# Prologue of a fused two-block transformer kernel: how the residual, the pool bias, the router weights and the small vectors are loaded

## The chip, the cores and the metric

The kernel runs on one core of a Trainium2 chip. A core has TensorE (PE in the views; its weight loads are PEld), VectorE (DVE), ScalarE (ACT), GpSimd (POOL) and SyncE (SP). SP and ACT issue the transfers here, each on a DMA queue of its own (q1 is SP's, q10 is ACT's), and 16 DMA engines serve both queues. The metric is the device time of the core in microseconds (us), the median over several executions.

## What is computed

One sequence of 256 tokens with 1024 channels in float32 goes through two blocks. Only the beginning of the first one is touched by the change:

```python
def pool_mixer(h, w, b, scale):      # trailing-window means minus the token, per group of 256 channels
    ...
    y = jnp.einsum('bsgc,gcd->bsgd', pooled, w) + b
    return y.reshape(B, S, D) * scale

x = x + pool_mixer(rms_norm(x, pool_norm[l]), pool_w[l], pool_b[l], pool_scale[l])   # layer 0
x = x + hier_moe(rms_norm(x, ffn_norm[l]), router_group_w[l], ..., w_gate[l], w_up[l], w_down[l])
```

`hier_moe` picks one of 4 groups and two of its 8 experts for each token. Layer 1 has multi-head latent attention in place of the pool mixer, and the same expert stage again. The second block (an S5 and an mLSTM branch, cross-attention to a memory `mem_2`, a convolutional feed-forward) follows. Each of the 64 experts has three matrices of 2 MB, which makes some 400 MB of the 512 MB that the kernel moves.

## The kernel before

**Slabs and the ring.** Weights come in slabs of up to 2 MB (128 partitions by 4096 floats). The ring `ring` in SBUF has 6 places; a slab `n` may be loaded (`place_free`, `placed`, L597; `rows`, L579) when the slab that held its place has been used up, which TensorE tells with the semaphore `slabs_done`. Three more slabs of each expert stage (`AHEAD`) go to other memory: one into `arena`, two in halves over X, XN and parts of `arena` (`load_ahead`, `load_over_x` L630, `load_over_sorting` L638). SP issues everything in program order, so a slab that must wait for its place holds back all that stands behind it.

**The prologue.** SP issues `x` into `X` (L538), seven small vectors (`vectors`, L545, of which each is some rows of 128 floats), `pool_w` (L548), the other small vectors, the S5 vectors (L551, L552), the memory (L560), the router's weights and biases of layer 0 (`router_loads`, L555 to L558). Then it waits for `vec2_loaded` and `pool_loaded`, and only then issues slab XK0 (L579) and the first five expert slabs (L597). ACT issues the constants (L1507), the band matrix `inverse_counts` (L1508), the pool bias and the pool scale, both broadcast to 128 partitions (L1509, L1510: 512 KB of writes each), and `ffn_gain` (L1512).

TensorE begins with `keep_busy` (L818, products that nothing reads), transposes the first vectors (L823), goes on with `keep_busy`, and multiplies the normed X with the band (L831, L832) and the result with `pool_w` (L841). DVE copies the transposed gains (L1928), forms XN (L1904), multiplies the product with the scale (L1943) and adds it to X (L1944). GpSimd has by then multiplied bias and scale (L2557) and added them to X (L2564, two instructions of 128x1024).

**Router and experts.** `turn(X)` (L751) makes 16 transposes of 128x128 blocks of X; DVE and ACT copy them with the gain into `hT` (L1913, L1532); the memory is turned in layer 0 as well; L868 multiplies `hT` with the router weights `rw`. The block that is transposed is the operand that a weight load brings in (PEld L751). DVE then picks experts, TensorE sorts the tokens with `XN_rows`, a view of XN with a step of 8 floats, as weights (`sort`, L899), and the expert loop starts: `gate_up` (L956), `turn_hid` (L972), `combine` (L985), `down` (L1000). L1029 is a set of products whose weights have one row.

Of the kernel before, what the change touches and what calls it, by code (L numbers as in the profile page):

```python
# [25 lines left out]
P = 128  # L26
T = 256
TT = T // P
D = 1024
# [55 lines left out]
def side_by_side(widths):  # L85
    at, cols = 0, {}
    for name, n in widths:
# [6 lines left out]
                                    ("iota", SLOTS), ("group", EXPERTS), ("causal_mask", P), ("eps", 1),  # L94
# [4 lines left out]
def constants():  # L99
# [22 lines left out]
    put("eps", np.full((P, 1), EPS))  # L122
# [18 lines left out]
VECTORS = (("pool_norm", 8), ("ffn_norm", 16), ("kv_in_norm", 8), ("attn_norm", 8), ("kv_norm", 2),  # L141
# [117 lines left out]
FIRST_VECTORS = 7  # L259
# [12 lines left out]
def key_tiles(batch):  # L272
# [25 lines left out]
    "proj_mm", "pool_biased",  # L298
# [23 lines left out]
def program(nc, a, out):  # L322
    with ExitStack() as ctx:
# [21 lines left out]
        ffn_gain = sbuf("ffn_gain", [P, 2, KD])  # L345
        PS = ctx.enter_context(nc.psum_tensor("PS", [P, 8, 512], F32))
# [23 lines left out]
        ident, ones, eps = cc("ident"), cc("ones"), cc("eps")  # L370
# [31 lines left out]
        pool_b = ar(13056, D)  # L402
# [4 lines left out]
        hTf = hT[:, :, :].rearrange("p k n -> p (k n)")  # L407
        slots = hTf[:, 0:2 * TOP_K * T].rearrange("p (v n) -> p v n", v=2)
# [128 lines left out]
        def _(sp):  # L537
            sp.dma_start(X[:, :, :], a["x"].rearrange("b (t p) d -> p (b t) d", p=P)).then_inc(s["x_loaded"], 16)  # L538
# [9 lines left out]
            sp.dma_start(pool_w, a["pool_w"].rearrange("a g (c p) d -> p (a g c) d", p=P)).then_inc(s["pool_loaded"], 16)  # L548
            vectors(VEC_PARTS[FIRST_VECTORS:], "vec2_loaded")
            for at, name in ((0, "s5_lam_re_2"), (S5J, "s5_lam_im_2")):  # L550
                sp.dma_start(s5_rows[at:at + S5J, :], a[name][0].rearrange("(j g) p -> j (g p)", g=2)).then_inc(s["s5_loaded"], 16)  # L551
            sp.dma_start(ldt2[32:32 + S5J, :], a["s5_log_dt_2"][0].rearrange("(j g) -> j g", g=2)).then_inc(s["s5_loaded"], 16)  # L552

            def router_loads(layer):
                sp.dma_start(rw[:, :, 0:GROUPS], a["router_group_w"][layer].rearrange("(k p) g -> p k g", p=P)).then_inc(s["row_loaded"], 16)  # L555
# [29 lines left out]
            def experts(layer, n0):  # L585
# [30 lines left out]
                def load_over_x():  # L616

                    name = ("ffn0", "ffn1")[layer]
                    sp.wait_ge(s["x_loaded"], 16 * (2 + 2 * layer))
# [116 lines left out]
        def _(pe):  # L736
# [8 lines left out]
            def turn(v, bank=4):  # L745

                for j in range(KD // 2):
                    for c in (2 * j, 2 * j + 1):
                        for t in range(TT):
                            at = (c % 2) * T + t * P  # L750
                            mm = pe.transpose(PS[:, bank + j, at:at + P], v[:, t, c * P:(c + 1) * P], ident)  # L751
# [71 lines left out]
            pe.transpose(PS[:, 0, 0:FIRST_ROWS], vec_rows[0:FIRST_ROWS, 0, :], ident[0:FIRST_ROWS, 0:FIRST_ROWS]).then_inc(s["vec_turned"], 1)  # L823


            keep_busy(7, 7)
# [8 lines left out]
            pe.wait_ge(s["pool_loaded"], 16 * 3)  # L835
            for g in range(N_POOL):
                pe.wait_ge(s["norm_hT_dve"] if g < 2 else s["norm_hT_act"], KD // 2)
                for t in range(TT):
                    o = PS[:, 2 * t + g // 2, (g % 2) * POOL_GD:(g % 2 + 1) * POOL_GD]
                    for c in range(2):  # L840
                        mm = pe.matmul(o, pl[:, 2 * g + c, t * P:(t + 1) * P], pool_w[:, 2 * g + c, :], start=(c == 0), stop=(c == 1))  # L841
# [3 lines left out]
            def moe(layer, name, n0):  # L845
# [9 lines left out]
                turn(X)  # L855
# [642 lines left out]
        def _(act):  # L1498
# [7 lines left out]

            act.dma_start(const[:, :], a["const"]).then_inc(s["const_loaded"], 16)  # L1507
# [1194 lines left out]
```

## Time and profile before

| | us |
|---|---|
| median of 3 runs (lowest, highest) | 1704.22 (1703.78, 1706.92) |
| the profiled execution: device time | 1701.31 |
| the profiled execution: span of its instructions | 1699.1 |
| PE busy | 1607.1 (95%) |
| DVE, ACT, POOL busy | 456.3, 234.3, 96.7 |
| moved by DMA | 512.48 MB, mean 302 GB/s |

The chain that ended last is TensorE for 63% and DMA for 30%; the DMA part is nearly all the wait for `in_w_up` slabs. The views below are read like this: the chain of waits gives start, length and engine with line of what the end of the program hung on; a stretch gives the busy time of each engine, PE's granted clock, the mean busy share of the 16 DMA engines (it can read slightly over 1) and GB/s.

### The profile page before, as it was taken

To read this page: it belongs to the slowest core of one execution; us is meant where nothing else is said; L and a number is where in the kernel's file an instruction comes from. 1 tells how busy PE (TensorE), PEld (TensorE's weight loads), DVE (VectorE), ACT (ScalarE), POOL (GpSimd) and SP (SyncE) were. 2 spreads that over 40 slices of the span, in tenths; PEclk is the share of its full clock that TensorE was granted. 3 is DMA by queue.
4 is the path that set the end of the run, shared out by engine and by line. 5 is a ranking of instruction groups with operands and counts; after the bars stand their busy time and mean duration, and the time that the engine had idled before them with its cause. 6 is when DMAs were issued, how large, how long until landed. Compare 5 with 4: busy or idle time off the path is not lost.

```text
span 1699.1 us, 22104 instructions
## 1 busy us (share of the span) xinstructions
PE 1607.1 (95%) x9079; PEld 1002.9 (59%) x9079; DVE 456.3 (27%) x982; ACT 234.3 (14%) x519; POOL 96.7 (6%) x165
## 2 busy tenths in 40 slices
PE   8999998888999999999998898899999998999998
PEld 7755544444446756745544444448578667688843
DVE  4311111111113323212111111116976202344411
ACT  4110100000002121101000000012122113100000
POOL 2200000000000000029200000000000000000000
PEclk9999999999999999999999999999999999999999
DMA  9999999999998643899999999999233541444400
GB/s 329 414 423 425 426 427 426 426 425 427 426 421 299 194 173 125 366 408 421 426 426 426 426 426 427 426 380 329 89 124 125 186 161 50 161 149 149 149 25 25
DMA packets 107944, 512.48 MB, mean 302 GB/s; under 512 B 17034, under 2 KB 46315, under 8 KB 74091
## 3 DMA queue, kind: packets, MB, share of 16 engines
q1 hardware_dynamic: 105595, 506.24, 74.3%
q10 hardware_dynamic: 2288, 5.40, 0.9%
q8 instruction: 41, 0.67, 0.2%
q14 instruction: 20, 0.16, 0.0%
HBM read 506.38 MB, written 5.24 MB: 301 GB/s over the span
## 4 chain that ended last, share of the span: by engine, by line
PE 63%; DMA 30%; DVE 4%; SPq 1%; ACT 1%; issue 1%; DVEq 0%; ACTq 0%
DMA ring<-in_w_up 29%; PE PS L956 15%; PE PS L1462 9%; PE PS L1000 5%; PE PS L1224 5%; PE PS L1474 4%; PE PS L1235 2%; PE PS L985 2%; PE PS L899 2%; PE PS L1400 2%; PE PS L1412 2%; PE PS L1389 2%; PE PS L1203 2%; PE PS L811 2%; PE PS L796 1%; DMA ring<-in_x_wkv 1%
## 5 line engine op out<-in xcount | busy, mean ns | idle before, releaser
L956 PE MATMUL PS<-ring,arena 128*64 128x256 f32 x3968 | 449.2, 381 | 54.6 <-DMA ring<-in_w_up 42.5
L956 PEld LDWEIGHTS PS<-ring,arena 128*64 128x64 f32 x3968 | 287.7, 137 | 236.4 <-DMA ring<-in_w_up 59.8
L1000 PE MATMUL PS<-ring,arena 128*64 128x512 f32 x992 | 226.6, 598 | 1.2 <-ACT arena L1641 1.2
L2098 DVE TENSOR_TENSOR arena<-PS,arena 128x256 f32<-128x256 f32 x64 | 27.2, 425 | 719.6 <-ACT arena L1633 719.6
L1000 PEld LDWEIGHTS PS<-ring,arena 128*64 128x64 f32 x992 | 66.2, 136 | 152.8 <-issue 151.3
L1462 PE MATMUL PS<-hT,ring 128*128 128x256 f32 x640 | 138.3, 379 | 0.0
L1462 PEld LDWEIGHTS PS<-hT,ring 128*128 128x128 f32 x640 | 121.6, 190 | 16.5
L985 PE MATMUL PS<-arena,hT 64*128 64x512 f32 x512 | 127.2, 615 | 1.2 <-ACT arena L1650 1.2
L1641 ACT ACTIVATE arena<-PS 128x256 f32<-128x256 f32 x64 | 24.6, 384 | 507.4 <-PE PS L972 507.4
L1224 PE MATMUL PS<-hT,ring 128*128 128x256 f32 x384 | 85.9, 385 | 0.0
L1650 ACT ACTIVATE arena<-PS 128x512 f32<-128x512 f32 x64 | 38.2, 597 | 306.2 <-PE PS L1000 306.2
L1224 PEld LDWEIGHTS PS<-hT,ring 128*128 128x128 f32 x384 | 73.7, 193 | 11.2 <-issue 1.1
L1474 PE MATMUL PS<-ring,arena 128*128 128x512 f32 x176 | 75.7, 592 | 0.0
L985 PEld LDWEIGHTS PS<-arena,hT 64*128 64x128 f32 x512 | 44.1, 186 | 39.9 <-issue 30.2
L1474 PEld LDWEIGHTS PS<-ring,arena 128*128 128x128 f32 x176 | 33.4, 190 | 41.7 <-issue 41.4
L2110 DVE SCALAR_TENSOR_TENSOR hT<-hT,arena 128x512 f32<-128x512 f32 x64 | 50.5, 789 | 0.4 <-PE PS L985 0.2
L2289 DVE SCALAR_TENSOR_TENSOR arena<-PS,VT,arena 128x255 f32<-128x255 f32 (+2 forms) x104 | 43.5, 476 | 1.1
L2284 DVE TENSOR_SCALAR arena<-PS,VT 128x256 f32<-128x256 f32 x48 | 23.0, 538 | 77.5 <-PE PS L1462 77.4
L2092 DVE COPY arena<-arena 128x512 f32 (+1 forms) x64 | 28.6, 447 | 29.2 <-issue 22.2
L972 PEld LDWEIGHTS PS<-const,arena 128*128 128x128 f32 x128 | 20.3, 206 | 24.8 <-issue 24.7
L899 PE MATMUL PS<-arena,XN 128*128 128x256 f32 x128 | 32.3, 409 | 0.9 <-DVE arena L2023 0.9
L899 PEld LDWEIGHTS PS<-arena,XN 128*128 128x128 f32 x128 | 31.2, 335 | 3.2 <-issue 2.9
(422 smaller groups left out, 1433.8 us busy)
## 6 DMA issues: line engine op xcount, KB each, us to landing
ring<-in_w_gate SPq DMA_DIRECT2D x62, 2048.0 KB, 25.5
ring<-in_w_up SPq DMA_DIRECT2D x62, 2048.0 KB, 25.6
ring<-in_w_down SPq DMA_DIRECT2D x62, 2048.0 KB, 24.6
ring<-in_f_w_up SPq DMA_DIRECT2D x22, 1024.0 KB, 6.7
ring<-in_w_in SPq DMA_DIRECT2D x9, 2048.0 KB, 19.1
ring<-in_f_w_down SPq DMA_DIRECT2D x5, 2048.0 KB, 7.9
arena<-in_w_gate SPq DMA_DIRECT2D x2, 2048.0 KB, 23.0
ring<-in_x_wkv SPq DMA_DIRECT2D x2, 2048.0 KB, 8.3
```

The source lines that it names most:

```text
L811: mm = pe.matmul(PS[:, 1, :], hT[:, k, t * P:(t + 1) * P], w[:, k, :], start=(k == 0), stop=(k == KD - 1))
L899: mm = pe.matmul(PS[:, 4 * half + c // 2, c % 2 * T:(c % 2 + 1) * T], XN_rows[:, t, c, :], sel[:, t, half * T:(half + 1) * T], start=(t == ...
L956: mm = pe.matmul(PS[half * WINDOW:(half + 1) * WINDOW, bank, m * half_f:(m + 1) * half_f], xw[bank][:, k, :], mat(k, F_EXP)[:, half * half ...
L985: mm = pe.matmul(PS[:, 4 + 2 * t + half, :], buf[rows, t * P:(t + 1) * P], y2[rows, :], start=first, stop=last, skip_group_check=True)
L1000: mm = pe.matmul(PS[half * WINDOW:(half + 1) * WINDOW, 3, :], hidT[:, w, k * WINDOW:(k + 1) * WINDOW], mat(k, D)[:, half * 512:(half + 1) ...
L1203: mm = pe.matmul(PS[:, 2 + 2 * half + t, :], oT[:, h, t * P:(t + 1) * P], w[:, h, :], start=(h == 0), stop=(h == HEADS - 1))
L1224: mm = pe.matmul(PS[:, bank + b, f % 2 * T:(f % 2 + 1) * T], w[:, k, f * P:(f + 1) * P], x[:, k, :], start=(k == 0), stop=(k == kx - 1))
L1462: mm = pe.matmul(PS[:, 2 * (j % 2) + h, f * T:(f + 1) * T], w[:, k, h, f * P:(f + 1) * P], x[:, k, :], start=(k == 0), stop=(k == KD - 1))
L1474: mm = pe.matmul(PS[:, 4 + 2 * t + half, :], gF[:, c, t * P:(t + 1) * P], w[:, c - 4 * j, half * 512:(half + 1) * 512], start=(c == 0), st ...
L1650: act.activation(y2, PS[:, 3, :], ACT.Copy).then_inc(g["y_sbuf"], 1)
L2110: dve.scalar_tensor_tensor(gates2, slots[:, 0, :], slot_of[:, w, bass.ds(linear(e, 1, 0), 1)], slots[:, 1, :], ALU.is_equal, ALU.mult).the ...
L2289: ins = dve.scalar_tensor_tensor(v, ps(f)[:, 0:T - back], taps[f][back], v, ALU.mult, ALU.add)
```

## The change

- `x` is loaded in two halves of one token tile each, the first by SP, the second by ACT, each the first entry of its queue. The constants and the band come after it on ACT's queue.
- Pool bias and pool scale are loaded as one row each. A row of ones (`warm`, a memset in hT) times the scale row gives the broadcast scale in PSUM (two products of 512 columns), which DVE copies to SBUF. A row of ones times the bias row starts the accumulation of the pool product (four products of 512 columns), to which L857 adds. The bias is so inside the product and is scaled with it; GpSimd's three instructions are gone.
- TensorE starts with 8 products of `warm` with itself. After the transposed vectors there are 10 `keep_busy` products (7 before).
- The router weights are loaded with channel `p*8+k` at partition p, part k, which makes each partition's data one run; so `turn(X)` takes its columns with a step of 8 (`X_rows`), in both layers. The gain comes from `ffn_gain` in that order, and `ffn_norm` leaves the list of vectors.
- The second list of vectors and the S5 vectors are issued behind XK0 and the first two expert slabs, and SP's wait before the first slab is gone.
- `eps` is a memset in place of a column of the constants.

```diff
-            sp.dma_start(X[:, :, :], a["x"].rearrange("b (t p) d -> p (b t) d", p=P)).then_inc(s["x_loaded"], 16)
+            sp.dma_start(X[:, 0, :], a["x"].rearrange("b (t p) d -> p (b t) d", p=P)[:, 0, :]).then_inc(s["x_loaded"], 16)
...
-                sp.dma_start(rw[:, :, GROUPS:], a["router_expert_w"][layer].rearrange("(k p) g -> p k g", p=P)).then_inc(s["row_loaded"], 16)
+                sp.dma_start(rw[:, :, GROUPS:], a["router_expert_w"][layer].rearrange("(p k) g -> p k g", p=P)).then_inc(s["row_loaded"], 16)
...
-            sp.wait_ge(s["vec2_loaded"], 16 * (len(VEC_PARTS) - FIRST_VECTORS))
-            sp.wait_ge(s["pool_loaded"], 16 * 3)
...
+                    if layer == 0 and j == SECOND_SLABS:
+                        second_vectors()
                     placed(j)
...
+                            part = v[:, t, c * P:(c + 1) * P] if rows is None else rows[:, t, c, :]
+                            mm = pe.transpose(PS[:, bank + j, at:at + P], part, ident)
...
-            pe.wait_ge(s["const_loaded"], 16)
-            keep_busy(7, 8)
+            pe.wait_ge(s["dve_step"], 2)
+            for _ in range(8):
+                pe.matmul(PS[:, 4, 0:P], warm, warm, start=True, stop=True)
+            pe.wait_ge(s["pool_loaded"], 16 * 2)
+            for half in range(2):
+                mm = pe.matmul(PS[:, 6 + half, :], warm[0:1, :], scale_row[:, half * 512:(half + 1) * 512], start=True, stop=True)
+            mm.then_inc(s["rows_spread"], 1)
+            for half in range(2):
+                for t in range(TT):
+                    pe.matmul(PS[:, 2 * t + half, :], warm[0:1, :], pool_b[:, half * 512:(half + 1) * 512],
+                              start=True, stop=False, skip_group_check=True)
+            pe.wait_ge(s["const_loaded"], 16)
             pe.wait_ge(s["vec_loaded"], 16 * FIRST_VECTORS)
...
-            keep_busy(7, 7)
+            keep_busy(4, 10)
...
-                turn(X)
+                turn(X, rows=X_rows)
...
-            act.dma_start(pool_b, a["pool_b"].rearrange("a g d -> (a g d)").partition_broadcast(P)).then_inc(s["pool_loaded"], 16)
-            act.dma_start(pool_scale, a["pool_scale"][0].partition_broadcast(P)).then_inc(s["pool_loaded"], 16)
+            act.dma_start(X[:, 1, :], a["x"].rearrange("b (t p) d -> p (b t) d", p=P)[:, 1, :]).then_inc(s["x_loaded"], 16)
+            act.dma_start(pool_b, a["pool_b"].rearrange("a g d -> a (g d)")).then_inc(s["pool_loaded"], 16)
+            act.dma_start(scale_row, a["pool_scale"]).then_inc(s["pool_loaded"], 16)
...
-            pool.wait_ge(s["norm_xn"], TT)
-            for t in range(TT):
-                pool.tensor_tensor(X[:, t, :], X[:, t, :], pool_b, ALU.add).then_inc(s["pool_biased"], 1)
```

TensorE's first instructions, before (L818 is `keep_busy`, L823 the transposed vectors, L831 the first band product):

```order
L818 MATMUL PS<-const 128x128 [waits const_loaded]
L818 MATMUL PS<-const 128x128 x7
L823 MATMUL PS<-const,arena 128x53 [waits vec_loaded]
L818 MATMUL PS<-const 128x128 x7
L831 MATMUL PS<-arena,XN 128x256 [waits band_loaded,norm_xn]
```

And after (L828 is the product of `warm`, L831 the scale row, L835 the bias row, L839 the transposed vectors, L847 the first band product):

```order
L828 MATMUL PS<-hT 128x128 [waits dve_step]
L828 MATMUL PS<-hT 128x128 x7
L831 MATMUL PS<-arena,hT 128x512 [waits pool_loaded]
L831 MATMUL PS<-arena,hT 128x512
L835 MATMUL PS<-arena,hT 128x512 x4
L839 MATMUL PS<-const,arena 128x37 [waits vec_loaded,const_loaded]
L824 MATMUL PS<-const 128x128 x10
L847 MATMUL PS<-arena,XN 128x256 [waits band_loaded,norm_xn]
```

Six products of 512 columns now stand ahead of the transposed vectors.

SP's queue from the memory to the third expert slab, before:

```order
L560 DMA arena<-in_mem 128x2x1024
L555 DMA arena<-in_router_group_w 128x8x4
L556 DMA arena<-in_router_expert_w 128x8x32
L557 DMA arena<-in_router_group_b 128x4
L558 DMA arena<-in_router_expert_b 128x32
L579 DMA ring<-in_x_wkv 128x8x384 [waits pool_loaded,vec2_loaded]
L597 DMA ring<-in_w_gate 128x4096
L597 DMA ring<-in_w_up 128x4096
L597 DMA ring<-in_w_gate 128x4096
```

And after, from `pool_w` on:

```order
L551 DMA arena<-in_pool_w 128x8x256
L566 DMA arena<-in_mem 128x2x1024
L561 DMA arena<-in_router_group_w 128x8x4
L562 DMA arena<-in_router_expert_w 128x8x32
L563 DMA arena<-in_router_group_b 128x4
L564 DMA arena<-in_router_expert_b 128x32
L582 DMA ring<-in_x_wkv 128x8x384
L600 DMA ring<-in_w_gate 128x4096
L600 DMA ring<-in_w_up 128x4096
L548 DMA arena<-in_mix_norm_g 8x128
L548 DMA arena<-in_s_d 4x128
```

The slabs follow the router's loads without a wait, and the vectors, which stood ahead of the memory, stand behind two expert slabs.

## Rows read from the trace of the kernel before

**Rows 1.** Chain of waits, first 60 us: start us, length us, what.

```profile
3.64 7.14 DMA arena<-in_mem_norm_g
11.17 3.29 PE PS L818 x14
14.46 0.58 PE PS L831 x2
19.84 6.91 PE PS L841 x32
26.75 2.90 PE PS L818 x26
29.65 3.60 PE PS L751 x32
46.00 8.01 PE PS L899 x32
58.33 7.06 PE PS L956 x64
```

**Rows 2.** Chain of waits, later: both expert stages' bounds, and layer 1's turn.

```profile
235.24 25.78 DMA ring<-in_w_up
507.02 14.01 DMA ring<-in_x_wkv
659.05 1.75 PE PS L751 x16
836.03 22.36 DMA ring<-in_w_up
```

**Rows 3.** Stretches: busy us of the engines, PEclk, DMA share, GB/s.

```profile
20.00:22.00 2.00, 2.00 (x11) 1.77 (x10) 0.00 (x0) 1.74 (x4) 2.00 (x2) 1.00 0.28 33
22.00:24.00 2.00, 2.00 (x11) 1.74 (x11) 0.23 (x2) 1.94 (x7) 2.00 (x1) 1.00 0.69 100
...
232.00:506.00 274.00, 247.46 (x1674) 125.03 (x1672) 37.57 (x77) 23.25 (x56) 0.00 (x0) 1.00 1.01 426
...
668.00:684.00 16.00, 14.40 (x66) 12.74 (x64) 9.09 (x41) 1.73 (x5) 0.00 (x0) 1.00 0.01 4
```

**Rows 4.** Timeline of SP's issues: start us, length, line, transfer.

```profile
87.66 0.43 SPq L638 DMA_DIRECT2D arena<-in_w_down  x1
99.67 0.33 SPq L597 DMA_DIRECT2D ring<-in_w_gate  x1
```

**Rows 5.** SP's own waits between 99 and 100 us.

```profile
SPq L597 <- PE PS L1000: 11.6, 1, 11.6
```

**Rows 6.** Landings, us from issue: issued at 87.66, 99.67, 643.62 and 0.75.

```profile
arena<-in_w_down SPq DMA_DIRECT2D x1, 1024.0 KB, 15.7
ring<-in_w_gate SPq DMA_DIRECT2D x1, 2048.0 KB, 8.6
ring<-in_w_up SPq DMA_DIRECT2D x1, 2048.0 KB, 7.9
const<-in_const ACTq DMA_DIRECT2D x1, 596.5 KB, 5.6
```

**Rows 7.** Timeline of PE and DVE in the prologue; x counts passes, two per product.

```profile
6.39 3.78 PE L818 MATMUL PS<-const 128*128 128x128 f32 x16 [6.39 <-DMA const<-in_const]
12.59 0.75 DVE L1904 TENSOR_SCALAR XN<-X,stat 128x1024 f32<-128x1024 f32 x1
26.58 3.06 PE L818 MATMUL PS<-const 128*128 128x128 f32 x26
```

**Rows 8.** One line's weight loads: ns lowest/median/highest, first and last start.

```profile
L1029 PEld LDWEIGHTS PS<-const,arena x16: 181/187/187, 1140.0 to 1141.7; 1*128 1x128 f32 x16
L899 PEld LDWEIGHTS PS<-arena,XN x128: 312/336/338, 46.0 to 708.4; 128*128 128x128 f32 x128
L751 PEld LDWEIGHTS PS<-const,X x48: 138/140/143, 29.5 to 660.4; 128*128 128x128 f32 x48
```

**Rows 9.** Timeline of DVE and POOL before the pool result is added.

```profile
23.94 0.16 DVE L1937 RECIPROCAL stat<-stat 128x1 f32<-128x1 f32 x1 [1.13 <-ACT stat L1523]
19.37 4.67 POOL L2564 TENSOR_TENSOR X<-X,arena 128x1024 f32<-128x1024 f32 x2
```

More of the change, by code:

```diff
@@ L368, in bc @@
             return v.to_broadcast([P, *shape])
-        ident, ones, eps = cc("ident"), cc("ones"), cc("eps")
+        ident, ones, eps = cc("ident"), cc("ones"), eps_at[:, 0:1]
         ssq, rms, rinv = stat[:, 0:2], stat[:, 2:4], stat[:, 4:6]
@@ L618, in load_over_x @@
                     name = ("ffn0", "ffn1")[layer]
-                    sp.wait_ge(s["x_loaded"], 16 * (2 + 2 * layer))
+                    sp.wait_ge(s["x_loaded"], 16 * (3 + 2 * layer))
                     sp.wait_ge(s["norm_xn"], TT * (SCALED.index(name) + 1))
@@ L743, in slab_wait, with turn @@
                     pe.wait_ge(loaded(n), slab_bytes_due(n))
-            def turn(v, bank=4):
+            def turn(v, bank=4, rows=None):
                 for j in range(KD // 2):
@@ L840, in _ @@
                     for c in range(2):
-                        mm = pe.matmul(o, pl[:, 2 * g + c, t * P:(t + 1) * P], pool_w[:, 2 * g + c, :], start=(c == 0), stop=(c == 1))
+                        mm = pe.matmul(o, pl[:, 2 * g + c, t * P:(t + 1) * P], pool_w[:, 2 * g + c, :], start=False, stop=(c == 1),
+                                       skip_group_check=True)
                     if g % 2:
@@ L1523, in norm, with router_gain @@
                     act.activation(rms[:, t:t + 1], ssq[:, t:t + 1], ACT.Sqrt, bias=eps, scale=1.0 / D).then_inc(s["norm_rms"], 1)
+            def router_gain(layer):
+                return lambda name, c: ffn_gain[:, layer, c:c + 1]
             def hT_upper(name, gains, at=0, dsts=(hT,), bank=4, col=vec):
@@ L1562, in norm_halves @@
                             half(t)
-            act.wait_ge(s["x_loaded"], 16)
+            act.wait_ge(s["dve_step"], 2)
+            act.wait_ge(s["x_loaded"], 32)
+            norm("pool")
             act.wait_ge(s["const_loaded"], 16)
-            norm("pool")
             act.wait_ge(s["vec_ready"], 1)
@@ L1592, in moe @@
                     act.wait_ge(s["hm_moved"], 2)
-                hT_upper(name, ["ffn_norm"], KD * layer)
+                act.wait_ge(s["gain_loaded"], 16)
+                hT_upper(name, ["ffn_norm"], col=router_gain(layer))
                 if layer:
@@ L1904, in norm, with router_gain @@
                         dve.tensor_scalar(XN[:, t, :], src[:, t, :], rinv[:, t:t + 1], None, ALU.mult).then_inc(s["norm_xn"], 1)
+            def router_gain(layer):
+                return lambda name, c: ffn_gain[:, layer, c:c + 1]
             def hT_lower(name, gains, at=0, dsts=(hT,), bank=4, col=vec):
@@ L1924, in scale_turned @@
                        .then_inc(s["h_scaled"], 1)
-            dve.wait_ge(s["x_loaded"], 16)
+            step(dve.memset(eps, EPS))
+            step(dve.memset(warm, 1.0))
+            dve.wait_ge(s["rows_spread"], 1)
+            dve.tensor_copy(pool_scale.rearrange("p (h n) -> p h n", h=2), PS[:, 6:8, :])
+            dve.wait_ge(s["x_loaded"], 32)
             dve.wait_ge(s["vec_turned"], 1)
-            dve.tensor_copy(VT[:, 0:FIRST_ROWS], PS[:, 0, 0:FIRST_ROWS]).then_inc(s["vec_ready"], 1)
+            dve.tensor_copy(VT[:, 0:FIRST_ROWS], PS[:, 5, 0:FIRST_ROWS]).then_inc(s["vec_ready"], 1)
             dve.wait_ge(s["vec_ready"], 1)
@@ L1952, in moe @@
                     dve.wait_ge(s["hm_moved"], 2)
-                hT_lower(name, ["ffn_norm"], KD * layer)
+                dve.wait_ge(s["gain_loaded"], 16)
+                hT_lower(name, ["ffn_norm"], col=router_gain(layer))
                 norm(name)
@@ L2554, in step @@
                 pool.wait_ge(s["pool_step"], steps[0])
-            pool.wait_ge(s["pool_loaded"], 16 * 3)
-            step(pool.tensor_tensor(pool_b, pool_b, pool_scale, ALU.mult))
             pool.wait_ge(s["s5_loaded"], 16 * 3)
```

45 lines of the change are left out of this document (22 added, 23 removed).

## The prediction, written before the changed kernel ran

> **What bounds the kernel now.** I read the chain of waits first, from the start to the second block, then the stretches for the DMA share, then SP's issues with their landings.
>
> Up to 232 us the chain is TensorE and the engines that feed it [rows 1]. From 235 us it is the wait for slabs [rows 2]: in the stretch from 232 to 506 us the 16 DMA engines are busy all the time and move 426 GB/s [rows 3]. Expert stage 0 thus ends when its slab stream ends, and the stage behind it begins with the landing of the slab issued at 507.02, 14.01 us later, at 521.0 [rows 2]. So a prologue counts there only by what it does to that stream. The stream has two possible masters: the moment it starts, and the moments at which TensorE gives back places of the ring. The narrowest such moment is at 99.67: SP had waited 11.6 us for TensorE's L1000 [rows 5], and the transfer issued before that one (87.66) landed 15.7 us later, at 103.4 [rows 4, 6]. The slab issued at 99.67 landed after 8.6 us, at 108.3, 4.9 us behind the one ahead of it, which is what 2 MB take at 426 GB/s [rows 3, 6]. A slab issued into an empty queue, at 643.62, took 7.9 us [rows 6]. So the stream has 8.6 - 7.9 = 0.7 us in hand at 99.67, and no more. A stream that starts earlier has nothing to carry beyond this point unless TensorE comes earlier too; and every us by which TensorE comes later, after the first 0.7, goes into the end of stage 0.
>
> In layer 1 there is nothing in hand: from 668 to 684 us the DMA engines do nothing (share 0.01) [rows 3], since the places wait for TensorE, and the stream bounds the chain again from 836 us [rows 2]. What TensorE loses between 657 and 684 us moves the whole second stage.
>
> **The slab stream's start.** Two broadcasts of 512 KB go: 1.05 MB at 426 GB/s are 2.5 us. The wait of SP goes: shares of 0.28 and 0.69 in two stretches of 2 us are 1.44 + 0.62 = 2.1 us of idle DMA [rows 3]. The router's short runs become long ones; the trace has no row of these alone, I put it between 0 and the 1.5 us that would fill the rest of those stretches. The vectors are only moved. Sum: the stream could start 4.6 to 6.1 us earlier, and no less than TensorE allows. The vectors land behind two slabs, before their first reader (behind L868, at some 37 us), so their move costs nothing; were they late by more than about 5 us, TensorE would stand behind L868.
>
> **TensorE's prologue.** Before, the transposed vectors are done at 11.17, 7 keep-busy products (14 passes) take 3.29 us, and the first band product starts at 14.46 in the chain [rows 1]. XN is ready at 12.59 + 0.75 = 13.34 [rows 7], 2.2 us behind the vectors, because DVE needs these first.
>
> After, TensorE first does 8 products without need of data, from about 1 us to 4.5 us (16 passes took 3.78 us at 6.39 [rows 7]). Then it waits for the two rows. They stand behind half of X on ACT's queue, with the other half of X beside it on SP's: 1 MB ahead of them. The constants, 0.6 MB with as much of X beside them, landed 5.6 us after 0.75 [rows 6], at 6.35. I take 6.2 us.
>
> Price of a product of 512 columns: 16 products of 256 columns take 6.91 us [rows 1], so 0.43 each, 0.86 for 512. That is at the full clock. A keep-busy product takes 3.06/13 = 0.235 us at 26.58, and 3.78/8 = 0.47 us at 6.39 [rows 7]: in the first 14 us TensorE runs at 1.2 GHz, not at 2.4, though the PEclk column reads 1.00. At the low clock 512 columns are 1.72 us. One row of weights is no cheaper than 128: L1029's 16 passes follow each other at (1141.7 - 1140.0)/15 = 0.11 us [rows 8].
>
> When does the clock rise? In the kernel before, near 14.6 us, 8.2 us after the first product and 3.8 us after work resumed from the pause before 10.8 (products behind 14.46 go at full price, those ahead do not [rows 1, 7]). Counted from the first product here this gives 9.3 us, from the resumption at 6.2 it gives 10.0, and if the first 8 products counted for nothing and 8.2 us were needed again, 14.4. I take 11, nearer to the first two.
>
> So: two scale products, 6.2 to 9.6 us. Four bias products: 1.4 us at the low clock do 0.8 of one, the other 3.2 cost 2.75 us, done at 13.75. Transposed vectors, 0.35 us: 14.1. DVE's XN, 2.2 us later: 16.3; 10 keep-busy products at 0.235 end at 16.5. The first band product comes at about 16.5 in place of 14.46: **2.1 us later**. Earlier X and statistics gain nothing, since DVE waits for the vectors, and these for the row products. DVE's own copy of the scale (1024 columns, from 9.6 us) ends before 14.1; it costs nothing unless it took over 4 us.
>
> **GpSimd's bias.** The two additions end at 19.37 + 4.67 = 24.04, and DVE's pool result starts behind them. But DVE also waits for ACT's memory statistics: its reciprocal starts at 23.94 and takes 0.16, so 24.1 [rows 9]. Both waits end together; removing one gains nothing. On TensorE too the 13 keep-busy products run up to the turn at 29.65 [rows 1]. So the 2.1 us pass on unchanged.
>
> **turn(X) with a step of 8.** L751's weight loads take 140 ns, and layer 1's 16 transposes 1.75 us, 0.109 each [rows 2, 8]. The one line that already loads weights with a step of 8, L899, has 336 ns [rows 8], and its 32 passes of 256 columns take 8.01 us, 0.250 each, where L841 with contiguous weights takes 6.91/32 = 0.216 [rows 1]. The first wait aside, L899's loads, not its columns, set 0.24 us. If a transpose of 128 columns is bound by the same load, 16 of them take 3.8 us in place of 1.75: **2.05 us more in each layer**. The lower bound is 0, if the load hides in part behind something that only L899 has. I take 2.05, for L899 is the only such row. In layer 0 the memory's turn and L868 stand behind it, in layer 1 L796 and L868, all in the chain.
>
> The Trainium skill has two sentences that part here. "TensorE: Matmul & The Clock Gate", section "LDWEIGHTS (loading the stationary operand)", lets the load's time hang on the number of columns alone; by that the turn would cost nothing more. "Advanced Engine Details and Errata", section "SBUF Cachelines", says that accesses need two hits on a line of 16 bytes for full speed; a step of 8 floats has one. Rows 8 side with the second.
>
> **The sum.** Stage 0: TensorE is late by 2.1 + 2.05 = 4.15 us at each return of a place; 0.7 is in hand; the stream ends 3.4 us later. The earlier start is all spent by 99.67. Layer 1: 2.05 us. Together 5.45 us. The profiled execution took 1701.31 us (span 1699.1), which becomes 1706.8; the median of 1704.22 lies 2.9 us over it, and becomes **1709.7**.
>
> **Rivals.**
> - *One-row products don't raise the clock.* Then all six cost 1.72: 6.2 + 10.3 = 16.5, vectors at 17.0, ten keep-busy products at 0.47: 21.7. The prologue is 7.2 us late, stage 0 is 8.6 later, sum 10.6: 1714.8. For it: no row has such products at the low clock.
> - *The clock is already up at 6.2 us.* Vectors at 6.2 + 5.2 + 0.35 = 11.75, band product at 14.1, 0.3 early. Stage 0: 2.05 - 0.3 - 0.7 = 1.05, layer 1 2.05, sum 3.1: 1707.3. Against it: 3.8 us of the same products followed by a pause did not do it before.
> - *The step of 8 is free.* Stage 0: 2.1 - 0.7 = 1.4: 1705.6.
> - *The stream's start is the master*, the side opposite to my forecast: if the ring has more in hand than I read at 99.67, the end of stage 0 follows the start. It decides from the point at which the slack there passes 4.15 us. Then -6 to -4.6 us, and +2.05 in layer 1: about 1700.8. For it: the whole of stage 0 past 232 us is DMA, and every byte or gap taken out ahead is real. Against it: SP's wait of 11.6 us for TensorE with only 8.6 us left to the landing.
>
> **Numbers.** Forecast 0.48, low clock 0.17, early clock 0.12, free step 0.10, stream 0.13. A measurement here can tell about 0.2% (3.4 us) from no change. Slower by more: forecast and low clock, 0.65. Within: early clock and free step, 0.22. Faster: 0.13. The range leaves out the stream case and the far end of the low clock: 1703.5 to 1715.
>
> **What would show it.** In the profile of the changed kernel: the first row product near 6.2 us, the band product near 16.5; turn(X) at 0.24 us a transpose in both layers; the first slab landing some 6 us earlier, but an idle DMA before the slab issued near 104 us; 521.0 becoming about 524.4; the second stage another 2 us later. I am wrong if the DMA never idles between 60 and 110 us, if the turn stays at 0.11, or if the band product comes before 14.5.

## The result, and the profile after

The changed kernel takes 1712.65 us (median of 9 runs, 1709.66 to 1715.59), the kernel before 1703.88 us (9 runs, 1702.81 to 1706.92). The ratio is 1.0054, 95% interval 1.0045 to 1.0062: 8.8 us slower, inside the range of the prediction and 3 us above its forecast.

The chain of waits of the changed kernel (start us, length us, what), beside [rows 1]:

```profile
1.76 4.55 DMA arena<-in_pool_scale
...
6.35 1.98 PE PS L831 x4
8.33 6.31 PE PS L835 x8
14.63 0.25 PE PS L839
14.88 4.40 PE PS L824 x20
19.28 0.43 PE PS L847 x2
...
31.43 2.90 PE PS L824 x26
34.33 3.51 PE PS L757 x32
...
50.58 8.04 PE PS L916 x32
58.62 4.32 PE PS L802 x20
62.94 1.87 PE PS L973 x15
64.81 1.15 issue
```

The first band product starts at 19.28 in place of 14.46. The distance from there to the turn (34.33; 29.65 before) and on to the sort (50.58; 46.0 before) is what it was: the 4.8 us of the first 19 pass on as 4.6 to 4.7. The two scale products (L831) cost 0.50 us a pass, the four bias products (L835) 0.79. The stretches of the same kernel (length, then busy us of PE, PEld, DVE, ACT, POOL, then PEclk, DMA share, GB/s) say why:

```profile
6.00:8.00 2.00, 1.65 (x4) 0.85 (x5) 0.00 (x0) 1.99 (x3) 0.00 (x0) 1.00 0.97 346
8.00:10.00 2.00, 2.00 (x4) 0.71 (x3) 1.22 (x1) 1.94 (x6) 0.00 (x0) 0.68 1.00 345
10.00:12.00 2.00, 2.00 (x4) 0.79 (x3) 0.00 (x0) 0.14 (x1) 0.00 (x0) 0.50 1.11 369
...
18.00:20.00 2.00, 2.00 (x13) 1.92 (x13) 0.00 (x0) 0.00 (x0) 0.00 (x0) 0.76 0.79 243
```

The granted clock is at full speed (2.4 GHz) when the row products begin, falls to half (1.2 GHz) in the middle of them, at 8.7 us, and is back only near 19 us. (Ahead of its first rise the PEclk column reads 1.00 as well; that the clock is really up at 6.35 us is seen from the 0.50 us a pass.) From 6.35 us on TensorE is busy all the time; what is unusual is that its products have one row.

At the narrow place, first SP's issue on the timeline, then SP's wait ahead of it, the landing (KB, us from issue), and the stretches around it:

```profile
105.87 0.33 SPq L600 DMA_DIRECT2D ring<-in_w_gate  x1
...
SPq L600 <- PE PS L1017: 11.6, 1, 11.6
...
ring<-in_w_gate SPq DMA_DIRECT2D x1, 2048.0 KB, 7.7
...
104.00:106.00 2.00, 2.00 (x14) 0.79 (x12) 0.00 (x0) 0.12 (x1) 0.00 (x0) 1.00 0.36 147
106.00:108.00 2.00, 2.00 (x22) 1.32 (x20) 0.00 (x0) 0.48 (x1) 0.00 (x0) 1.00 0.73 164
```

The place comes back at 105.87 (99.67 before, [rows 4]) and its slab lands at 113.6 (108.3 before, [rows 6]). The DMA engines run dry here: the stream now waits for TensorE. In the kernel before they were busy in the same stretch:

```profile
104.00:106.00 2.00, 2.00 (x22) 1.35 (x20) 0.00 (x0) 0.00 (x0) 0.00 (x0) 1.00 1.00 426
```

At the end of expert stage 0 the wait that answers to [rows 2] is

```profile
512.08 15.04 DMA ring<-in_x_wkv
```

which lands at 527.1, 6.1 us later than before.

### The profile page after: what moved, and what is told of

Read it like the earlier page. It is cut to its first block, busy times and chain, and to the rows that moved or that the text cites. A ratio compares the mean times of both kernels' runs of the same rounds, so it can differ in the third digit from the quotient of the medians.

```text
span 1710.0 us, 22138 instructions
## 1 busy us (share of the span) xinstructions
PE 1621.5 (95%) x9097; PEld 1010.7 (59%) x9097; DVE 458.2 (27%) x985; ACT 234.2 (14%) x519; POOL 90.0 (5%) x162
## 4 chain that ended last, share of the span: by engine, by line
PE 63%; DMA 30%; DVE 4%; ACT 1%; issue 1%; SPq 1%; ACTq 0%; DVEq 0%
DMA ring<-in_w_up 29%; PE PS L973 15%; PE PS L1479 9%; PE PS L1017 5%; PE PS L1241 4%; PE PS L1491 4%; PE PS L1252 2%; PE PS L1002 2%; PE PS L916 2%; PE PS L1417 2%; PE PS L1429 2%; PE PS L1406 2%; PE PS L817 2%; PE PS L1220 2%; DMA ring<-in_x_wkv 1%; PE PS L802 1%
```

## The experiments

All ratios are to the kernel before, run beside the experiment, with 95% intervals; each trace is one profiled execution. The table puts side by side where the narrowest place comes back (SP's issue that is at 99.67 in [rows 4]), when x_wkv lands, and the time.

| kernel | place back | x_wkv lands | difference | ratio |
|---|---|---|---|---|
| before | 99.7 | 521.0 | 421.3 | |
| router weights and step of 8 alone | 100.3 | 522.2 | 421.9 | 0.9995 |
| broadcasts, vectors first, even rows | 100.5 | 522.7 | 422.2 | 1.0007 |
| the same, bias early | 101.2 | 522.0 | 420.8 | 1.0002 |
| 128 rows, vectors first, even rows | 101.3 | 522.6 | 421.3 | 1.0028 |
| "bias early" with the memory first and the router behind a slab | 101.4 | 522.8 | 421.4 | 1.0016 |
| broadcasts, vectors first | 103.1 | 524.7 | 421.6 | 1.0018 |
| bias behind the vectors | 104.1 | 525.4 | 421.3 | 1.0021 |
| after, even rows | 104.3 | 526.4 | 422.1 | 1.0048 |
| before, 20 more busy products | 104.7 | 526.6 | 421.9 | 1.0030 |
| 128 rows | 104.8 | 526.8 | 422.0 | 1.0041 |
| row products alone | 105.8 | 526.6 | 420.8 | 1.0050 |
| after | 105.9 | 527.1 | 421.2 | 1.0054 |
| broadcasts in after | 106.6 | 527.9 | 421.3 | 1.0036 |

The difference stays between 420.8 and 422.2 while the place moves by 7 us and the first slab's issue ranges from 15.6 to 23.6 us. The ratio follows the place only roughly (101.2 has 1.0002, 101.3 has 1.0028): the medians contain more than stage 0.

### The row products alone, and their opposite

The kernel before with the one-row products and nothing else of the change:

```diff
-            act.dma_start(pool_b, a["pool_b"].rearrange("a g d -> (a g d)").partition_broadcast(P)).then_inc(s["pool_loaded"], 16)
...
+            act.dma_start(pool_b, a["pool_b"].rearrange("a g d -> a (g d)")).then_inc(s["pool_loaded"], 16)
...
+                    pe.matmul(PS[:, 2 * t + half, :], ones[0:1, :], pool_b[:, half * 512:(half + 1) * 512],
+                              start=True, stop=False, skip_group_check=True)
```

> The kernel before with one part alone: the one-row products for pool scale and pool bias ahead of the transposed vectors, GpSimd's additions and the two broadcasts gone; loads of X, router, vectors and SP's wait as before. Theory A: 5.2 us of products at the full clock, 10.3 at the low one, stand ahead of the transposed vectors (11.2 before); the band product comes 3 to 8 us later than 14.5, and the time is 2.5 to 8 us above before. Theory B: the slab stream is untouched, so the time is that of before within 1 us.

Measured: 1713.1 us, ratio 1.0050 (1.0033 to 1.0067). Its chain, and one stretch:

```profile
6.46 3.78 PE PS L818 x16
10.25 1.94 PE PS L824 x4
12.19 5.22 PE PS L828 x8
...
14.00:16.00 2.00, 2.00 (x3) 0.79 (x3) 0.00 (x0) 0.00 (x0) 0.07 (x1) 0.50 1.01 395
```

The clock rose at 10.3 us, about when the row products began, and fell at 13.7 in the midst of them, until 20.5. This part alone loses as much as the whole change (1.0050 and 1.0054, with overlapping intervals).

The changed kernel with the broadcasts and GpSimd's additions put back:

```diff
-                    pe.matmul(PS[:, 2 * t + half, :], warm[0:1, :], pool_b[:, half * 512:(half + 1) * 512],
-                              start=True, stop=False, skip_group_check=True)
...
-            act.dma_start(pool_b, a["pool_b"].rearrange("a g d -> a (g d)")).then_inc(s["pool_loaded"], 16)
...
+            act.dma_start(pool_b, a["pool_b"].rearrange("a g d -> (a g d)").partition_broadcast(P)).then_inc(s["pool_loaded"], 16)
...
+                pool.tensor_tensor(X[:, t, :], X[:, t, :], pool_b, ALU.add).then_inc(s["pool_biased"], 1)
```

> The changed kernel with one part undone: pool bias and pool scale are again broadcast by DMA (behind the band on ACT's queue) and added by GpSimd; no one-row products; all else as changed. Theory A (the six one-row products, priced at the low clock, make TensorE late, and stage 0 follows TensorE): the transposed vectors come near 9 us, the first band product between 11.5 and 13.7 us in place of 19.3, places return 1 to 3 us earlier than in the kernel before, and the time is 0 to 3 us below before (1701 to 1704). Theory B (the slab stream with the vectors behind two slabs is what became slower, since SP stood 11.4 us on one vector transfer): the stream keeps its shape, and the time stays some 6 to 9 us above before.

Measured: 1711.45 us, ratio 1.0036 (1.0024 to 1.0049): little came back. The band product is at 13.1 and the turn at 29.2, but the timeline of PE shows a wait that the changed kernel does not have:

```profile
40.85 0.96 PE L882 MATMUL PS<-const,arena 128*128 128x128 f32 x3 [4.40 <-DMA arena<-in_f_conv_b]
41.91 0.31 PE L886 MATMUL PS<-const,arena 48*128 48x48 f32 x1
42.15 6.08 PE L802 MATMUL PS<-arena,ring 128*128 128x256 f32 x14
```

With TensorE on time, the second vectors behind two slabs are late. SP adds to it: `f_conv_b` is issued only at 36.38 us, behind an issue of `f_conv_w` that holds SP for 11.5 us (more on it below), and no run tells the two shares apart. The wait also lowers the clock (from 37.6 to 47.8 us), so that L802's 14 passes take 6.08 us in place of 3.29, and the sort starts at 52.8, later than in the changed kernel. So the change holds two causes, and one hides the other: TensorE that comes late does not notice vectors that come late.

### The step of 8 alone

```diff
-                sp.dma_start(rw[:, :, 0:GROUPS], a["router_group_w"][layer].rearrange("(k p) g -> p k g", p=P)).then_inc(s["row_loaded"], 16)
+                sp.dma_start(rw[:, :, 0:GROUPS], a["router_group_w"][layer].rearrange("(p k) g -> p k g", p=P)).then_inc(s["row_loaded"], 16)
...
-                turn(X)
+                turn(X, rows=X_rows)
```

> The kernel before with one part alone: router weights in contiguous rows, turn(X) with a step of 8 floats in both layers, gain from ffn_gain. My prediction's step: 2.05 us more in each layer's turn, 3.4 us in all. What the trace of the changed kernel says (1.76 us for 16 passes, as before): nothing, the time is that of before within 1 us, perhaps 1 us less for the shorter router loads.

Measured: 1704.55 us, ratio 0.9995 (0.9985 to 1.0005). The weight loads (ns lowest/median/highest) and layer 1's turn in the chain:

```profile
L754 PEld LDWEIGHTS PS<-const,X x48: 139/192/207, 29.3 to 663.2; 128*128 128x128 f32 x48
...
661.80 1.78 PE PS L754 x16
```

and in the changed kernel

```profile
L757 PEld LDWEIGHTS PS<-const,X x16: 185/188/193, 666.4 to 668.1; 128*128 128x128 f32 x16
...
666.71 1.76 PE PS L757 x16
```

A load is 50 ns longer than in [rows 8], but the 16 transposes take 1.76 to 1.78 us as before ([rows 2]: 1.75). The forecast of 3.8 is refuted.

### A delay of TensorE by itself

```diff
-            keep_busy(7, 7)
+            keep_busy(7, 27)
```

> The kernel before with 20 more keep-busy products behind the transposed vectors, nothing else: TensorE is late by 20 x 0.235 = 4.7 us (up to 9.4 if the clock stays low) in the prologue, the slab stream starts as before. If stage 0's stream has only 0.7 us in hand (my step), the slab whose place returned at 99.67 is issued at 104.4 and lands about 4 us later, and the time is 4 us (up to 8) above before. If the start of the stream is the master, the time is within 1 us of before.

Measured: 1710.61 us, ratio 1.0030 (1.0019 to 1.0042).

```profile
11.31 8.42 PE PS L818 x54
...
51.01 8.01 PE PS L899 x32
```

Sort and place are 5.0 us late, the slab behind the place lands at 112.6, 4.3 late: 0.7 are absorbed there, as read from [rows 6]. At the end of the stage nothing of these 0.7 is left: x_wkv lands at 526.6, 5.6 late.

### 128 rows in place of one

The same number of products of 512 columns in the same places, over 128 rows of constants. This kernel and the next leave out the pool bias and use a scale of one, so they compute something else; only their times and traces are of use.

```diff
-                mm = pe.matmul(PS[:, 6 + half, :], warm[0:1, :], scale_row[:, half * 512:(half + 1) * 512], start=True, stop=True)
+                mm = pe.matmul(PS[:, 6 + half, :], warm, hTf[:, 128:640], start=True, stop=True)
...
-                    pe.matmul(PS[:, 2 * t + half, :], warm[0:1, :], pool_b[:, half * 512:(half + 1) * 512],
+                    pe.matmul(PS[:, 2 * t + half, :], warm, hTf[:, 640:1152],
```

> The changed kernel with its six one-row products replaced by six products over all 128 rows of constants, with as many columns and in the same place (the pool bias is left out and the scale is one; the edit leaves out that part of the computation). TensorE waits for the same two rows of data as before. Theory A (it is the one-row products that let TensorE's granted clock fall at 8.7 us and keep it low until 19 us): the clock stays up from about 5 us on, the six products take 0.86 us each at most, the first band product comes at 14 to 15 us in place of 19.1, the place comes back near 101 us in place of 105.9, and the time is 1704 to 1706, ratio to the kernel before 1.000 to 1.001. Rival B (the clock falls because of the wait ahead of these products, from 4.5 to 6.3 us, whatever follows it): the low stretch stays, band product at 19 us, ratio 1.005. Rival C (the loss of the kernel lies in something behind the prologue, such as the vectors behind the slabs or the arrival of data): band product early, but the ratio stays at 1.004 to 1.005.

Measured: 1711.79 us, ratio 1.0041 (1.0026 to 1.0055), the number of rival C. Chain, then timelines of DVE and POOL:

```profile
6.36 3.78 PE PS L832 x4
10.14 3.62 PE PS L836 x8
...
13.94 2.43 PE PS L824 x20
...
38.95 1.09 DVE L1996 COPY arena<-arena 128x8 f32<-128x8 f32 x1
...
38.22 1.81 POOL L2638 MEMSET arena<- 128x2048 f32 x1
```

In this execution the clock rose at 10.4 us, not at 5.3, and then it stayed up through the products: band product at 16.4, 2.9 us ahead of the changed kernel's. Two things took 2 us back ahead of the sort (49.8). DVE's copy of 8 columns ended at the end of GpSimd's memset, which waits for the late vectors: 1.09 us in place of 0.17. And TensorE's wait behind it brought a low clock from 44.5 to 47.9. The next kernel also takes those away: the second vectors stand ahead of the memory again, in even pieces (below).

```diff
+            second_vectors()
             sp.dma_start(memt, a["mem_2"].rearrange("b (t p) d -> p (b t) d", p=P)).then_inc(s["mem_loaded"], 16)
```

> The changed kernel with 128-row products in place of the one-row products (the pool bias is left out and the scale is one) and in addition the second vectors ahead of the memory and cut to multiples of 16 rows. Theory A (of the 3.0 us that the 128-row products gained up to the turn of X, 2 were given back before the sort because the vectors landed at 37 us: GpSimd's memset of 1.81 us, which waits for them, held DVE's copy of 8 columns for 1.09 us in place of 0.17, and the longer wait of TensorE let its clock fall at 44.5): the band product comes at 16.2 and the turn at 31.3 as there, the copy takes 0.17 us, no low stretch at 44, the sort starts at 47.6 to 48.2, the place comes back at 101.2 to 102, time 1705 to 1707.5, ratio 1.0005 to 1.002. Rival (the 128-row products gain nothing that lasts): place near 104.8, ratio 1.004.

Measured: 1708.14 us, ratio 1.0028 (1.0016 to 1.0039).

```profile
6.44 1.98 PE PS L833 x4
8.42 3.43 PE PS L837 x8
...
12.04 2.43 PE PS L825 x20
...
8.00:10.00 2.00, 2.00 (x6) 0.80 (x6) 1.22 (x1) 1.94 (x6) 0.00 (x0) 1.00 0.97 327
```

Up to the band product this pair with the changed kernel is clean, but for the values that are multiplied (constants in place of the rows of data): the clock is up from 4.4 us in one and 5.3 in the other, the first four passes take 1.98 us in both. Over 128 rows the bias products then take 3.43 us and the 20 busy passes 2.43; over one row 6.31 and 4.40. The difference, 2.88 + 1.97 = 4.85 us, is the whole delay of the band product (19.28 against 14.46). Theory A holds for the clock. The rival that it falls for the wait ahead of these products, whatever follows, is out: TensorE waits here too (1.67 us in place of 1.38), and the clock stays up. A longer wait does lower it: in the kernel with the second vectors first (below) TensorE stands from 4.8 to 8.3 us, and the clock falls at 8.0, as that kernel's stretch shows:

```profile
8.00:10.00 2.00, 1.67 (x8) 1.63 (x9) 1.11 (x3) 1.94 (x6) 0.00 (x0) 0.50 1.00 389
```

So a wait with one-row products behind it ended here as a long wait did. The sort starts at 45.8, 0.2 before that of the kernel before, yet the place comes back 1.7 us late behind a pause of 1.23 us at 60.0 (below), and the time (1.0028, 4.8 us) is longer than that explains.

### Bias behind the vectors

The four bias products stand in the place of the ten keep-busy products:

```diff
-                    pe.matmul(PS[:, 2 * t + half, :], warm[0:1, :], pool_b[:, half * 512:(half + 1) * 512],
-                              start=True, stop=False, skip_group_check=True)
...
-            keep_busy(4, 10)
+            for half in range(2):
+                for t in range(TT):
+                    pe.matmul(PS[:, 2 * t + half, :], warm[0:1, :], pool_b[:, half * 512:(half + 1) * 512],
+                              start=True, stop=False, skip_group_check=True)
```

> The changed kernel with the four bias products moved behind the transposed vectors, in the place of the ten keep-busy products; the two scale products stay ahead. Theory A (one-row products at the low clock cost 1.72 us each, and what stands ahead of the vectors delays DVE's normalised input): the vectors are transposed some 4 to 7 us earlier, at 9 to 11 us, XN is ready near 13, but the four bias products then take 6.9 us at the low clock and end at 16.5 to 18, so the band product comes at 16.5 to 18 in place of 19.1, and the products behind it run at the low clock for longer: time 1709 to 1712, ratio 1.003 to 1.005. Rival (the delay of the vectors is the whole cost, the clock none): the band product comes at 14 us and the ratio is 1.001 or less.

Measured: 1707.98 us, ratio 1.0021 (1.0011 to 1.0030).

```profile
8.77 7.12 PE PS L840 x8
15.89 1.15 PE PS L846 x2
```

The eight passes take 0.89 us each, and the band products run at the low clock too (until 21.9), so the turn starts at 34.1, only 0.2 earlier than in the changed kernel. The clock is the cost, not the place in the order. The time, however, is 4.7 us shorter than the changed kernel's, of which the place return in the traces shows 1.8.

### SP's stall, and the vectors in even pieces

```diff
             m = min(n - done, P - (at + done) % P)
+            if m > 16:
+                m -= m % 16
```

> The changed kernel with every transfer of a small vector that has over 16 rows cut so that its first piece has a multiple of 16 rows (127 rows become 112 and 15). Nothing else is changed. Theory A (TensorE's late place returns set the end of stage 0, SP's issues don't): SP's stall of 11.4 us at the transfer behind the one of 127 rows shrinks to under 2 us, the gate slab behind it is issued 9 to 10 us earlier, near 25 us, but the place return stays near 105.9 us and the time stays within 1 us of the changed kernel's, ratio 1.005. Rival (the stall of SP costs the stream real time): the slab issued near 106 goes out earlier, ratio 1.002 or less. Rival of the cause of the stall: if cutting 127 rows does not change it, the stall belongs to something else, such as the two slabs queued ahead of the vectors.

Measured: 1713.46 us, ratio 1.0048 (1.0032 to 1.0065). SP's timeline in the changed kernel, then in this one:

```profile
21.51 11.71 SPq L548 DMA_DIRECT2D arena<-in_f_conv_w  x2
...
34.90 0.42 SPq L600 DMA_DIRECT2D ring<-in_w_gate  x1
```

```profile
21.25 1.16 SPq L550 DMA_DIRECT2D arena<-in_f_conv_w  x3
...
24.54 0.42 SPq L602 DMA_DIRECT2D ring<-in_w_gate  x1
```

Since `ffn_norm` left the list, `f_conv_w` falls into pieces of 127 and 5 rows, and the issue behind the one of 127 holds SP for 11.4 us. Cut evenly, the stall is gone, the third expert slab is issued 10.4 us earlier, and the time does not move: an earlier stream is worth nothing while TensorE returns the place late. In the kernel before, where the piece has 111 rows, SP is not held (both issues in 1.12 us). The Trainium skill, "DMA: Bandwidth & Descriptors", section "Why a DMA increments its semaphore by 16 and not by 1", says that the number of engines that serve a transfer divides its slowest dimension, which leaves one engine for 127 rows. That the stall comes and goes with the 127 rows fits it; how long an issue behind such a transfer takes it does not say, and no view here shows the 16 engines one by one.

The same in a prologue that is on time, first without, then with even pieces (both with broadcasts, and the second vectors ahead of the memory):

```diff
+            second_vectors()
             sp.dma_start(memt, a["mem_2"].rearrange("b (t p) d -> p (b t) d", p=P)).then_inc(s["mem_loaded"], 16)
...
-                    if layer == 0 and j == SECOND_SLABS:
-                        second_vectors()
```

> The kernel with broadcast rows and GpSimd's additions (the one that measured 1711.5), but with the second small vectors issued ahead of the memory and the router's loads, where the kernel before has them; SP's wait ahead of the slabs stays removed. Theory A (there the 4.4 us of TensorE at 40.9 us, for vectors behind the slabs, and the low clock that follows, were the whole loss): no wait at L882, the place returns near 99.5 us, the clock stays up, time 1703 to 1705, ratio 0.999 to 1.001. Rival B (the broadcasts or the early transfers themselves cost something more): ratio 1.002 or over. Rival C (the earlier start of the stream, some 4 us, is worth something once TensorE is on time): 1701 or less, ratio 0.998 or less.

> The kernel with broadcast rows and the second vectors ahead of the memory, and in addition every small vector's first piece cut to a multiple of 16 rows. Theory A (the piece of 127 rows, which exists only since ffn_norm left the vectors, held SP for 6.4 us there and so brought the memory at 22.6 us in place of 20.95; ACT's statistics, DVE's pool result and TensorE's turn follow it): SP's stall falls under 1 us, the memory lands by 18.5 us, the turn of X starts at 29 to 29.6 in place of 31.1, no low clock follows, the place comes back at 98.5 to 99.8, time 1703 to 1705, ratio 0.998 to 1.001. Rival (the memory's landing is set by the bytes ahead of it): it stays at 22 us and the ratio at 1.002. Rival (the low clock behind the turn comes for a reason of its own): turn early, but the ratio over 1.001.

Measured: 1707.69 us, ratio 1.0018 (1.0008 to 1.0027), and 1705.31 us, ratio 1.0007 (0.9996 to 1.0018). SP and PE without even pieces, then the chain with them:

```profile
8.78 6.68 SPq L548 DMA_DIRECT2D arena<-in_f_conv_w  x2
...
31.14 3.15 PE L756 MATMUL PS<-const,X 128*128 128x128 f32 x16 [3.71 <-DVE X L1961]
```

```profile
12.71 8.09 DMA arena<-in_mem
...
29.35 3.79 PE PS L758 x32
```

Without them the stall of SP brings the memory at 22.6 us, ACT's statistics and DVE's pool result follow, TensorE waits 3.71 us for X and turns at the low clock. With them the turn is at 29.4. The memory landed at 20.8, not by 18.5 as I expected: the bytes ahead of it count too.

### Two attempts at a gain

GpSimd's product of bias and scale starts at the landing of the scale, and the additions behind it may come earlier (the diff is against the kernel before this one):

```diff
-            pool.wait_ge(s["pool_loaded"], 16 * 3)
+            pool.wait_ge(s["s5_small"], 16 * 2)
```

> The kernel before this one, with the pool weights on a semaphore of their own, so that GpSimd's product of bias and scale starts with the landing of the scale (13.9 us) and not of the pool weights (15.8), and its additions end some 1.9 us earlier, near 21.4. Theory A (TensorE's place returns set the end of stage 0, and in this prologue GpSimd's additions and the memory's statistics bound the turn of X): the turn starts at 27.5 to 28.5, the place comes back at 97.5 to 99, the slab behind it lands at 107 to 107.6, and the time is 1701.5 to 1704, ratio 0.9985 to 1.000. Rival (with TensorE earlier the stream's start, near 20 us, becomes the bound): the place comes back early but the slab lands no earlier than 108, ratio 1.000. Rival (TensorE, idle for longer ahead of the turn, loses its clock there): low stretch near 30 us, ratio 1.001 or more.

Measured: 1704.6 us, ratio 1.0002 (0.9992 to 1.0012). The turn did not come earlier (29.8), since the memory landed at 21.2 and DVE waits for ACT's statistics as well, as [rows 9] shows for the kernel before. Then the memory ahead of the second vectors, and the router behind XK0 and the first expert slab:

```diff
+                    if layer == 0 and j == 1:
+                        router_loads(0)
                     placed(j)
```

> The kernel with the early bias additions, but with the memory issued ahead of the second vectors (its issue comes at 4.2 us in place of 12.4) and the router's loads behind the first two slabs of the stream (in their old place they held SP from 13.6 to 22 us, and from 20 to 24 us the DMA engines are busy for 0.32 of the time). Theory A (the turn of X is bound by the memory's landing at 21.2 us through ACT's statistics, the slab behind the narrow place by both the stream's start and TensorE's place return): the memory lands at 17 to 19 us, the turn starts at 27 to 28.5, the first slab is issued by 14 us and lands by 22, the place comes back at 97.5 to 99.5 in place of 101.2, the slab behind it lands at 106 to 107.5 in place of 109.2, and the time is 1700.5 to 1703, ratio 0.998 to 0.9995. Rival (SP or TensorE then stands for the router's rows behind two slabs): the router's products start later than 34 us, ratio 1.001 or more. Rival (an earlier stream takes from the vectors and the memory what it gains itself): turn at 29.7 as before, ratio 1.000.

Measured: 1706.28 us, ratio 1.0016 (1.0006 to 1.0025). SP's issue of the router weights and PE's first product with them, on the timelines:

```profile
18.14 7.37 SPq L564 DMA_DIRECT2D arena<-in_router_expert_w  x1
...
33.52 3.82 PE L878 MATMUL PS<-arena,hT 128*128 128x36 f32 x32 [1.46 <-DMA arena<-in_router_expert_b]
```

The turn is 1.3 us earlier (28.4 in place of 29.8), but the router's rows land at 33.5 and TensorE waits for them: the first rival. No version here beats the kernel before.

## Why the prediction was right or wrong

- **What bounds the kernel: right.** The place came back 6.2 us late, its slab landed 5.3 late (6.2 - 0.7 = 5.5 by the working), the stage ended 6.1 late. The table shows the same rule over 7 us. The 0.7 us in hand is right only for that one slab, as the added busy products show too; at the end of the stage the table's differences scatter around that of the kernel before, so the 0.7 that the sum takes off was not there.
- **The stream's start: right.** The first slab went out 4.8 us earlier (4.6 to 6.1 forecast) and nothing of it was left at 62 us, where the slab that landed at 62.7 before lands at 62.6. It was SP's stall that ate it: with even pieces the same slab lands at 58.3, and the time is the same. An earlier start that is kept changed nothing either.
- **The vectors behind slabs: right only for this kernel.** The condition that the prediction named is real: with TensorE on time it stood 4.4 us there. The stall of SP was in no term.
- **TensorE's prologue: right in sign, the step on the clock failed.** The rows were there at 6.35 (6.2 forecast). I had the clock rise at 11 us and stay up; it rose at 5.3, ahead of the row products, and fell at 8.7 in their midst. No rival had this: "already up" had the scale products nearly right (1.72 us by its working, 1.98 measured), "don't raise the clock" was nearest in cause, at 7.2 us. Measured: 4.8 us in place of 2.1. That one row is no cheaper than 128 held (four passes take 1.98 us over one row and over 128), but the row it was read from, L1029, has products of a single column and could show nothing of it; and I did not carry the question over to what the clock makes of such products.
- **GpSimd's additions: right.** They are gone, and the turn is 4.7 us late as the band product is 4.8 late.
- **The step of 8: wrong.** The term of 2.05 us per layer is 0.0. L899's 0.24 us a pass belongs to passes of 256 columns behind loads of 336 ns; for 128 columns the loads are 188 ns and do not set the pace of 0.11. The row that I chose was the only one with a step, but it differed from the turn in more than the step. What the Trainium skill, "Advanced Engine Details and Errata", section "SBUF Cachelines", says of full speed is seen in the load's length (188 ns in place of 140), and not in the time.
- **The sum.** 5.45 us came from one term too small by 2.7 and one too large by 2.05 twice. In stage 0 they nearly cancel (4.15 forecast at the place, 4.6 measured at the sort); the rest of the 6.2 lies in the first expert product, 8.63 us in place of 7.06, of which the pause at 64.8 is 1.15. In layer 1, where the step was to cost 2.05, the first expert product starts at 692.66 in place of 684.96, 1.6 us more than at the end of stage 0; the turn is as before, and the 1.6 us lie in a stretch of low clock from 633.4 to 636.8. That the time fell in the range is in part luck: with its own two terms as measured the sum would be 4.8 - 0.7 = 4.1 us (4.8 without the 0.7), and the other 4 to 4.7 of the 8.8 come from what it had no term for.
- **What stays open.** The spans of the two traces differ by 10.9 us (the medians by 8.8). 6.1 are there when stage 0 ends and 1.6 more come ahead of layer 1's experts. Then 1.3 us go with the last `in_w_up` slab of the second stage (27.04 us in the chain in place of 25.79, without a cause that I can name), and some 2 come behind it, where the changed kernel spends more time at the low clock: between 100 and 1690 us it has four stretches of 3.4 to 6.8 us, the kernel before two of 3.4. But the kernel with the step of 8 alone has four as well, at the median of the kernel before. I can't say that the late stage brings them. For the same reason it is open why the kernel with the bias behind the vectors is 4.7 us faster than the changed one, and why the one with 128 rows and the vectors first loses 4.8 us with its place 1.7 late.

## What to carry to other kernels

A product that is used to save a transfer is not free for the engine that the program hangs on: put it where TensorE has slack, or give it all 128 rows where its clock matters (here that kept the clock up, and gained no time over the kernel before). Before removing or moving a transfer, find the narrowest place return of the weight stream; here what came earlier than that place was worth nothing, and what came later counted in full. And two delays in one prologue don't add: undoing one of them lays bare the other, so undo them together as well as one by one.

## What the hardware showed that was not expected

- **One-row products do not keep the clock up.** Six products of 512 columns, 12 passes back to back with PE busy 2.00 of 2.00 us: the granted clock fell 2.4 us after the first began (3.4 us with the row products alone, 10.25 to 13.7) and stayed at half for 10.2 us (6.8). The same columns over 128 rows, of constants, kept it at full speed.
- **A memset on GpSimd can hold an 8-column copy on DVE**: 1.09 us in place of 0.17, ended together with the memset (40.03). The Trainium skill, "SBUF — State Buffer", section "SBUF: two separate sides", names an exclusive port that both share; this row fits it. So do two rows of the changed kernel with even pieces, where the memset overlaps a DVE instruction of 1024 columns and both take longer than elsewhere (1.81 and 0.75 us). It was not tried by itself.

```profile
36.91 2.28 POOL L2636 MEMSET arena<- 128x2048 f32 x1
...
37.55 2.18 DVE L1928 TENSOR_SCALAR XN<-X,stat 128x1024 f32<-128x1024 f32 x1
```

- **A pause of TensorE without a visible cause**, 1.0 to 1.2 us some 14 passes into the first expert product (at 64.8 in the changed kernel, 63.7 and 60.0 in the two with 128 rows, none in the other traces). It stays open.
